# Three rounds of sixteen experts on one core: gate and up weights stored one behind the other, modulation loads spread over twelve experts, tokens' weights computed behind the first expert's rows

## The chip, the cores and the metric

The kernel runs on 1 core of one Trainium2 chip. All data are float32. The metric is the device time of one execution in microseconds (us), lower is better.

## The reference

`x` is 512 tokens of 1024 features. A first block (gated delta rule, spatial gating unit, output projection, layer norm) is followed by a hierarchical mixture of experts; a second model of two layers follows, each with an attention mixer (forgetting attention, then latent attention) and again a mixture of experts. So the mixture of experts runs three times, each time as

```python
def hier_moe(h, w_grp, b_grp, w_rt, b_rt, w_gate, w_up, w_down):
    t = h.reshape(T, D)                                  # 512 x 1024
    g_prob = softmax(t @ w_grp + b_grp)                  # 4 groups, the best is taken
    e_logits = (t @ w_rt + b_rt).reshape(T, 4, 4)        # 4 experts in a group, the two best
    w = softmax(e_top) * g_top                           # two weights per token
    a = einsum('td,edf->tef', t, w_gate)                 # 16 experts, 1024 -> 256
    u = einsum('td,edf->tef', t, w_up)
    hidden = silu(a) * u * combine[..., None]
    return einsum('tef,efd->td', hidden, w_down)         # 256 -> 1024
```

In the second model a layer's six modulation vectors (shift, scale and gate, before and behind the mixer) are `silu(c) @ w_ada + b_ada`, 6 x 1024 values.

## The kernel before, in words

The program is a row of `nc.Block`s. In each of them the five engines (PE for matmuls, DVE, ACT, POOL, and SP, which only issues DMAs) run programs of their own, which wait for one another by semaphores. At the end of a block all five meet: none begins the next block before the last has finished this one, SP included. The trace names such a wait by the line of the block (`PEq L1292` is the one of the mixture of experts).

`moe` (line 1231) is one block with two programs for each engine, one behind the other, with no meeting between them. The first (lines 1293 to 1577) projects the mixer's output, normalises, computes the router's logits and from them, on DVE, which tokens stand in which of 128 slots of each expert: chains of small operations `route`, `pick`, `rows`, and at last `weight` (lines 1524 to 1547), 18 links that wait for one another. `weight` makes each token's two weights `w1`, `w2`, and index lists that are read only behind the experts. It holds two exponentials on ACT (`gexp`, `dif`, lines 1417 to 1420).

The second program goes over the 16 experts, `body(e, par, pair)` for each engine. PE does for expert e: `gate_up` (line 1610, 8 float32 matmuls of 512 columns, gate in columns 0 to 255, up in 256 to 511; the trace counts each float32 matmul twice), then `down` of expert e-1 (line 1619), then `turn_h` (line 1615). The first two experts' rows are turned by PE (`turn_x`, line 1602) and copied from PSUM by ACT and DVE (`keep_x`, line 1626); the others' by DVE (line 1843). POOL fetches an expert's rows in four indirect DMAs of 1 KB pieces (`load_quarters`, line 1875). ACT issues the loads of expert e+2's gate and up weights when `gate_up` of e has ended (`load_gate_up`, line 1788), that of its down weights one step later, and the store of the results of e-1 into `y_rows` (`store_y`, line 1779).

The weights lie in a ring of four slots: `ring[0]` and `ring[1]` take gate and up (4096 floats in each partition), `ring[2]` and `ring[3]` take down. In a partition of `ring[0]` gate and up alternate: for each of 8 values of k, 256 floats of gate and then 256 of up:

```python
act.dma_start(ring[par][:, :].rearrange("p (k g n) -> p k g n", k=KD, g=2)[:, :, i, :],
              w[:, bass.ds(e, 1), :, :].rearrange("p e k n -> p (e k) n"))
```

In DRAM the 8 x 256 floats that a partition takes from one matrix are one run of 8 KB. The load of one matrix therefore writes 8 runs of 1 KB in each partition. The other big loads have runs of 2 KB (`w_in` and the like), 4 KB (down weights) and, for one matrix (`mla_w_ukv`), 8 KB.

SP has little to do during the experts. In the first two of the three rounds it loads what the modulation of the next layer needs (`modulation_loads`, line 1218): small rows, six blocks of 512 KB from `ada_part`, and `ffn_norm`, 512 KB. Each is held back until `gate_up` of one expert has ended: experts 1 to 6 and 7. DVE adds `b_ada` to them at experts 10 to 13 (`BIAS_AT`). Then SP issues the next stage's first two pieces of weights into `ring[0]` and `ring[1]`, behind `gate_up` of experts 14 and 15. The next stage (class `Combine`, line 1911) fetches each token's two results from `y_rows` by indirect DMAs on POOL (line 1971), adds them on DVE (line 2069), sums the modulation on PE (lines 1982 and 1988), normalises, turns the tokens on PE (line 2007) and projects them (line 2363 behind the first round, line 2611 behind the second).

Of the kernel before, what the change touches and what calls it, by code (L numbers as in the profile page):

```python
# [17 lines left out]
ALU = mybir.AluOpType  # L18
# [101 lines left out]
def build(nc, D, OUT, stop=None):  # L120
# [19 lines left out]
    with ctx:  # L140
# [61 lines left out]
        def rows8(w):  # L202
            return w.rearrange("(p k) n -> p k n", p=P)
# [4 lines left out]
        def plan_experts(gate, up, down):  # L208

            for e in range(NE):  # L210
                gu = [(lambda s, i=i: s[:, :].rearrange("p (k g n) -> p k g n", k=KD, g=2)[:, :, i, :], rows8(w[e]))
                      for i, w in enumerate((gate, up))]
                dn = [(lambda s: s[:, 0:KF * DM].rearrange("p (k n) -> p k n", k=KF), rows(down[e]))]
                W.plan(gu, e % 2, by_loop=e >= 2)
                W.plan(dn, 2 + e % 2, by_loop=e >= 2)
# [1015 lines left out]
        def moe(outT, gain, shift, gate_w, up_w, down_w, group_w, group_b, expert_w, expert_b, x_tok, y_in, early, late=None, mod=None):  # L1231
# [47 lines left out]
            dv_n += [("bias", i) for i in range(4)] if mod is not None else []  # L1279
            BIAS_AT = NE - 6  # L1280
            stage([("sum", j) for j in range(6)] + [("turned", 0, 0), ("turned", 0, 1), ("sum", 6), ("turned", 1, 0), ("turned", 1, 1), ("sum", 7)] +
# [10 lines left out]
            with nc.Block() as block:  # L1292
# [89 lines left out]
                def _(act):  # L1382
# [20 lines left out]
                    for t in tiles:  # L1403
# [6 lines left out]
                        if t == 2:  # L1410
# [5 lines left out]
                                                 bcast(ident[:, :].rearrange("p (s n) -> p s n", s=NQ).unsqueeze(2), P, NQ, NQ, P // NQ), ACT.Copy), "spread")  # L1416
                    DV.wait(act, ("weight", 1))
                    AC.done(nc.scalar.activation(gexp, gexp, ACT.Exp), "gexp")
                    DV.wait(act, ("weight", 4))
                    AC.done(nc.scalar.activation(dif, dif, ACT.Exp), "dif")  # L1420

                @block.vector
                def _(dve):
# [99 lines left out]

                    link = chain(DV, dve, "weight")
                    groups = lg3[:, :, 0:NG]
                    gx = gexp.rearrange("p (t n) -> p t n", t=T)
                    link(V.reduce_max(gm, groups, X_AXIS))
                    link(V.tensor_tensor(gx, groups, bcast(gm.unsqueeze(2), P, T, NG), ALU.subtract))
                    link(V.tensor_tensor(four(prod2), four(O12), bcast(lg3[:, :, NG:nrt].unsqueeze(1), P, 2, T, NE), ALU.mult))
                    link(V.reduce_sum(sel, prod2.rearrange("p (a n) -> p a n", n=NE), X_AXIS))  # L1530
                    link(V.tensor_tensor(dif, sel[:, T:2 * T], sel[:, 0:T], ALU.subtract))
                    AC.wait(dve, "gexp")
                    link(V.reduce_sum(gsum, gx, X_AXIS))
                    link(V.reciprocal(gp, gsum))
                    AC.wait(dve, "dif")
                    link(V.tensor_scalar_add(gm, dif, 1.0))
                    link(V.reciprocal(gm, gm))
                    link(V.tensor_tensor(w1, gp, gm, ALU.mult))
                    link(V.tensor_tensor(w2, w1, dif, ALU.mult))
                    c3 = cmpx.rearrange("p (x n) -> p x n", x=N_EXTRA)  # L1540
                    link(V.tensor_tensor(c3, bcast(incl.unsqueeze(1), P, N_EXTRA, NE), bcast(e_idx[:, 0:N_EXTRA].unsqueeze(2), P, N_EXTRA, NE), ALU.is_le))
                    link(V.reduce_sum(eidf[:, 0:N_EXTRA], c3, X_AXIS))
                    link(V.tensor_copy(eidf[:, N_EXTRA:N_EXTRA + 1], incl[:, NE - 1:NE]))
                    link(V.tensor_copy(ctl, eidf))
                    link(V.tensor_scalar(sel, rowsf, float(N_EARLY * P), FAR, ALU.is_lt, ALU.mult))
                    link(V.tensor_tensor(sel, sel, rowsf, ALU.add))
                    link(V.tensor_copy(rows_late, sel))

                @block.gpsimd
# [32 lines left out]
                yg = half(buf[2][:, 0:2048], DM)  # L1582
                w_gu = [ring[i][:, :].rearrange("p (k n) -> p k n", k=KD) for i in range(2)]
                w_dn = [ring[2 + i][:, 0:KF * DM].rearrange("p (k n) -> p k n", k=KF) for i in range(2)]
# [17 lines left out]
                def turn_x(eng, e, par, pair):  # L1602
# [5 lines left out]
                    last.then_inc(M_xT.sem, 1)  # L1608

                def gate_up(e, par):  # L1610
                    for k in range(KD):
                        last = nc.tensor.matmul(bank[2 + par][:, :], xgT[par][:, k, :], w_gu[par][:, k, :], start=(k == 0), stop=(k == KD - 1))  # L1612
                    last.then_inc(M_gu.sem, 1)
# [31 lines left out]
                extra_is = work[:, 3 * 4096 + 2048:3 * 4096 + 2048 + T * P]  # L1645
                extra_gu = halves_of_ring[:, :].rearrange("p (k n) -> p k n", k=KD)
                extra_dn = work[:, 2 * 4096 + 2 * DM:2 * 4096 + 4 * DM].rearrange("p (k n) -> p k n", k=KF)
# [10 lines left out]
                def extra_pe(x):  # L1658
                    nc.tensor.wait_ge(E_is, 2 * T * x + 2 * T)
                    for k in range(KD):  # L1660
                        for t in range(T):
                            last = nc.tensor.matmul(bank[k // 4][:, (k % 4) * P:(k % 4 + 1) * P], eighth(x_tok[:, t, :], k),
                                                    extra_is[:, t * P:(t + 1) * P], start=(t == 0), stop=(t == T - 1))
                    last.then_inc(E_pe, 1)
                    nc.tensor.wait_ge(E_in, 48 * x + 48)
                    nc.tensor.wait_ge(E_act, 3 * x + 1)
                    nc.tensor.wait_ge(E_dve, 4 * x + 1)
                    for k in range(KD):
                        last = nc.tensor.matmul(bank[2][:, :], xgT[0][:, k, :], extra_gu[:, k, :], start=(k == 0), stop=(k == KD - 1))
                    last.then_inc(E_pe, 1)  # L1670
                    nc.tensor.wait_ge(E_dve, 4 * x + 2)
                    for k in range(KF):
                        last = nc.tensor.transpose(bank[4][:, k * P:(k + 1) * P], h_tok[0][:, k * P:(k + 1) * P], ident[:, :])
                    last.then_inc(E_pe, 1)
                    nc.tensor.wait_ge(E_dve, 4 * x + 3)
                    for h in range(2):
                        for k in range(KF):
                            last = nc.tensor.matmul(bank[5 + h][:, :], hT[0][:, k, :], extra_dn[:, k, span(h)], start=(k == 0), stop=(k == KF - 1))
                    last.then_inc(E_pe, 1)

                def extra_act(x):
                    e = nc.scalar.value_load(ctl[0:1, bass.ds(x, 1)], min_val=0, max_val=NE - 1)
                    row = bass.ds(x * P + N_MAIN * P, P)
                    for i, w in enumerate((gr, ur)):
                        nc.scalar.dma_start(halves_of_ring[:, :].rearrange("p (k g n) -> p k g n", k=KD, g=2)[:, :, i, :],
                                            w[:, bass.ds(e, 1), :, :].rearrange("p e k n -> p (e k) n")).then_inc(E_in, 16)
# [71 lines left out]
                @block.sync  # L1758
                def _(sp):
                    W.issue(sp)  # L1760
                    assert W.issued == ids[4]
                    W.issued += 2 * NE - 4
                    if mod is not None:
                        DV.wait(sp, ("weight", N_WEIGHT - 1))
                        modulation_loads(sp, mod, lambda i: sp.wait_ge(M_gu.sem, v(M_gu, i + 1)))
                    W.issue(sp, 2)
                mod_loads = loads[0]

                @block.scalar
                def _(act):  # L1770
# [17 lines left out]
                    def load_gate_up(e, par):  # L1788
                        for i, w in enumerate((gr, ur)):
                            act.dma_start(ring[par][:, :].rearrange("p (k g n) -> p k g n", k=KD, g=2)[:, :, i, :],  # L1790
                                          w[:, bass.ds(e, 1), :, :].rearrange("p e k n -> p (e k) n")).then_inc(W.landed[par], 16)
# [4 lines left out]
                    def body(e, par, pair, first=False, free=False, no_y=False, tail=False, last=False):  # L1796
# [15 lines left out]
                        if not first:  # L1812
                            store_y(e - 1, 1 - par)
                    keep_x_act(0, 0)
                    body(0, 0, 0, first=True, free=True)
                    body(1, 1, 0, free=True, no_y=True)
# [9 lines left out]
                @block.vector  # L1826
                def _(dve):
                    def keep_y_dve(e, par, pair, early=False):
                        dve.wait_ge(M_down.sem, v(M_down, e))
# [16 lines left out]
                    def body(e, par, pair, first=False, early=False, last=False):  # L1846
# [10 lines left out]
                        if mod is not None and BIAS_AT <= e < BIAS_AT + 4:  # L1857
# [3 lines left out]
                            DV.done(nc.vector.tensor_tensor(part, part, b_ada[32 * i:32 * i + 1, :], ALU.add), ("bias", i))  # L1861
                    keep_x_dve(0, 0)
                    body(0, 0, 0, first=True)
                    body(1, 1, 0, early=True)
# [1057 lines left out]
```

## Time and profile before

| | before |
|---|---|
| runs | 2174.18, 2176.12, 2182.51 us; median 2176.12 |
| profiled execution | 2177.57 us, span 2175.8 us |
| mean granted TensorE clock | 0.977 |
| PE busy | 2073.0 us (95%) |
| DVE / ACT / POOL busy | 964.6 / 488.3 / 273.9 us |
| DMA | 363.32 MB in 208486 packets; mean 167 GB/s |

The profile is of the profiled execution. Idle PE time is not the whole loss in this kernel: a matmul at the lower of the clock's two levels counts as busy.

### The profile page before, as it was taken

The numbers are of one execution on the slowest core, as the hardware profiler recorded it, in microseconds if no ns is written. First come the engines' busy times: TensorE is split into PE (matmuls) and PEld (weight loads), VectorE is DVE, ScalarE is ACT, GpSimd is POOL, SyncE is SP. The second block draws the span as 40 slices with busy tenths as digits, with TensorE's granted clock in tenths as the row PEclk, the third lists the DMA queues.
The fourth block names the chain that finished last, engine by engine and source line by source line (L and its number), as shares of the span: only waits on it lengthen the run. The fifth ranks groups of instructions, "written<-read, shape, count | busy, mean of one in ns | idle before, by whom it ended". The sixth has DMA issues, their size and how long they took to land. (4 is left out here: it accounts for less than half of the span.)

```text
span 2175.8 us, 20699 instructions
## 1 busy us (share of the span) xinstructions
PE 2073.0 (95%) x7718; PEld 1159.7 (53%) x7718; DVE 964.6 (44%) x1696; ACT 488.3 (22%) x1086; POOL 273.9 (13%) x348
## 2 busy tenths in 40 slices
PE   8999999999999999999899999989999999999995
PEld 4444445488884445444445468544445568644442
DVE  2445445445553124334454656253353467434333
ACT  1111111043441001101331146220004446420000
POOL 1000000010002000334200000013331000003333
PEclk9999999999999999999998999999999999999998
DMA  5223365410012124799735920148994120045996
GB/s 174 93 94 126 135 245 217 156 41 2 1 53 102 65 92 155 253 376 379 267 121 199 323 111 1 39 144 307 374 379 164 62 98 2 3 153 172 369 374 258
DMA packets 208486, 363.32 MB, mean 167 GB/s; under 512 B 27580, under 2 KB 129240, under 8 KB 208128
## 3 DMA queue, kind: packets, MB, share of 16 engines
q1 hardware_dynamic: 87568, 174.13, 22.9%
q10 hardware_dynamic: 105696, 157.30, 20.5%
q0 software_dynamic: 15120, 30.53, 4.1%
q8 instruction: 64, 1.05, 0.2%
q14 instruction: 38, 0.31, 0.0%
HBM read 335.60 MB, written 43.52 MB: 174 GB/s over the span
## 5 line engine op out<-in xcount | busy, mean ns | idle before, releaser
L1612 PE MATMUL bank<-ring,work 128*128 128x512 f32 x768 | 345.7, 604 | 21.7 <-DVE work L1628 11.6
L1612 PEld LDWEIGHTS bank<-ring,work 128*128 128x128 f32 x768 | 145.0, 194 | 189.8 <-issue 177.1
L1877 POOL DMA_INDIRECT work<-x_rows,small x168 | 172.9, 1029 | 288.9 <-DVE work L1843 212.6
L1623 PE MATMUL bank<-ring_halves,work 128*128 128x512 f32 x384 | 172.9, 593 | 4.0 <-DVE work L1637 4.0
L423 PE MATMUL bank<-featT,ring 128*128 128x512 f32 x384 | 171.3, 600 | 4.3 <-DMA ring<-in_w_in 4.3
L1313 PE MATMUL bank<-ring,work 128*128 128x512 f32 x384 | 171.3, 607 | 2.9 <-PEq L2139 1.9
L2363 PE MATMUL bank<-ring,featT 128*128 128x512 f32 x384 | 169.9, 604 | 1.6 <-DVE small L2452 1.6
L1634 DVE TENSOR_TENSOR work<-work,bank 128x256 f32<-128x256 f32 x48 | 20.2, 421 | 306.0 <-ACT work L1631 306.0
L2363 PEld LDWEIGHTS bank<-ring,featT 128*128 128x128 f32 x384 | 74.1, 195 | 94.3 <-issue 92.5
L1313 PEld LDWEIGHTS bank<-ring,work 128*128 128x128 f32 x384 | 74.1, 195 | 94.0 <-issue 94.0
L1623 PEld LDWEIGHTS bank<-ring_halves,work 128*128 128x128 f32 x384 | 72.9, 190 | 94.9 <-issue 94.9
L423 PEld LDWEIGHTS bank<-featT,ring 128*128 128x128 f32 x384 | 72.3, 193 | 86.6 <-issue 82.3
L1631 ACT ACTIVATE work<-bank 128x256 f32<-128x256 f32 x48 | 18.4, 383 | 429.0 <-PE bank L1612 429.0
L522 PE MATMUL bank<-ring,featT 128*128 128x512 f32 x256 | 110.4, 593 | 0.9 <-PEq L405 0.9
L2197 PEld LDWEIGHTS bank<-work,featT 128*128 128x128 f32 x640 | 88.6, 192 | 24.8 <-issue 14.4
L2189 PE MATMUL bank<-work 65*128 65x128 f32 (+7 forms) x256 | 90.4, 438 | 0.1
L2197 PE MATMUL bank<-work,featT 128*128 128x65 f32 x640 | 86.0, 265 | 0.1
L1843 DVE STREAM_TRANSPOSE work<-work 128x1024 f32<-128x1024 f32 x42 | 85.1, 2025 | 0.0
L1030 PE MATMUL bank<-ring,featT 128*128 128x512 f32 x192 | 83.3, 593 | 1.0 <-PEq L796 1.0
L522 PEld LDWEIGHTS bank<-ring,featT 128*128 128x128 f32 x256 | 48.6, 190 | 61.3 <-issue 61.3
L279 DVE SCALAR_TENSOR_TENSOR ring_halves<-ring_halves,ismall 128x1024 f32<-128x1024 f32 x48 | 61.6, 1282 | 30.2 <-DMA ring_halves<-in_w_ada 26.4
L2215 ACT ACTIVATE featT<-bank,small 128x128 f32<-128x128 f32 (+3 forms) x128 | 73.2, 572 | 5.0 <-DVE small L2252 2.7
(442 smaller groups left out, 2784.8 us busy)
## 6 DMA issues: line engine op xcount, KB each, us to landing
ring<-in_w_in SPq DMA_DIRECT2D x16, 2048.0 KB, 12.6
ring<-in_moe_w_gate ACTq DMA_DIRECT2D x28, 1024.0 KB, 8.6
ring<-in_moe_w_up ACTq DMA_DIRECT2D x28, 1024.0 KB, 11.9
ring_halves<-in_moe_w_down ACTq DMA_DIRECT2D x28, 1024.0 KB, 12.0
ring_halves<-in_w_ada SPq DMA_DIRECT2D x48, 512.0 KB, 6.7
y_rows<-work ACTq DMA_DIRECT2D x48, 512.0 KB, 10.3
ring<-in_expert_w_gate ACTq DMA_DIRECT2D x14, 1024.0 KB, 9.8
ring<-in_expert_w_up ACTq DMA_DIRECT2D x14, 1024.0 KB, 12.8
```

Source lines behind the costliest of these rows:

```text
L423: last = nc.tensor.matmul(bank[b % 4][:, :], w[:, k, (b % 4) * P:(b % 4 + 1) * P], featT[:, k, :], start=(k == 0), stop=(k == KD - 1))
L522: last = nc.tensor.matmul(uv_bank(j)[:, :], featT[:, k, t * P:(t + 1) * P], w[:, k, :], start=(k == 0), stop=(k == KD - 1))
L1030: last = nc.tensor.matmul(zg_bank(j)[:, :], featT[:, k, t * P:(t + 1) * P], w[:, k, :], start=(k == 0), stop=(k == KD - 1))
L1313: last = nc.tensor.matmul(bank[j % 4][:, :], outT[:, k, t * P:(t + 1) * P], w[:, k, :], start=(k == 0), stop=(k == KD - 1))
L1612: last = nc.tensor.matmul(bank[2 + par][:, :], xgT[par][:, k, :], w_gu[par][:, k, :], start=(k == 0), stop=(k == KD - 1))
L1623: last = nc.tensor.matmul(bank[5 + h][:, :], hT[par][:, k, :], w_dn[par][:, k, span(h)], start=(k == 0), stop=(k == KF - 1))
L1843: nc.vector.transpose(xgT[par].rearrange("p k (s b) -> p s k b", s=NQ), xg[par].rearrange("p (s a k) -> p s k a", s=NQ, k=KD)).then_inc(M_ ...
L1877: nc.gpsimd.indirect_dma_start(out=xg[par][:, s * QD:(s + 1) * QD], out_offset=None, in_=x_quarters, in_offset=bass.IndirectOffsetOnAxis(a ...
L2189: PE.done(nc.tensor.matmul(bank[i % N_S][:, 0:(t + 1) * P], qT[:, t * P:(t + 1) * P], kT[:, 0:(t + 1) * P], start=True, stop=True), ("S", i))
L2197: last = nc.tensor.matmul(bank[6 + h % 2][:, t * DVO:(t + 1) * DVO], pT[j % 2][:, s, :], v[:, s, h, :], start=(s == 0), stop=(s == t))
L2215: AC.done(nc.scalar.activation(sx[i % 4][:, 0:n], bank[i % N_S][:, 0:n], ACT.Exp, bias=mx[:, i:i + 1], scale=1.0 if q_root is None else q_ ...
L2363: last = nc.tensor.matmul(f_bank(j)[:, :], featT[:, k, t * P:(t + 1) * P], w[:, k, :], start=(k == 0), stop=(k == KD - 1))
```

## The change

Three things. Gate and up are stored one behind the other in a slot (2048 floats of gate, then 2048 of up), so a matmul's moving operand is two runs of 256 floats that lie 2048 floats apart, and a load writes one run of 8 KB in each partition. The modulation loads are held back to experts 1, 2, 4, 6, 7, 9 and 11 (before: 1 to 7), the additions of `b_ada` to experts 12 to 15, and the second of the next stage's two pieces is issued only when the last result of the odd experts has been stored. The chain `weight` with its two exponentials moves from the first program's end into the second, behind `keep_x` of expert 0.

```diff
@@ plan_experts
-                gu = [(lambda s, i=i: s[:, :].rearrange("p (k g n) -> p k g n", k=KD, g=2)[:, :, i, :], rows8(w[e]))
+                gu = [(lambda s, i=i: s[:, :].rearrange("p (g k n) -> p g k n", g=2, k=KD)[:, i, :, :], rows8(w[e]))
@@ moe
-            BIAS_AT = NE - 6
+            BIAS_AT = NE - 4
@@ moe, first program of ACT
-                    DV.wait(act, ("weight", 1))
-                    AC.done(nc.scalar.activation(gexp, gexp, ACT.Exp), "gexp")
-                    DV.wait(act, ("weight", 4))
-                    AC.done(nc.scalar.activation(dif, dif, ACT.Exp), "dif")
@@ moe, first program of DVE
-                    link = chain(DV, dve, "weight")
-                    groups = lg3[:, :, 0:NG]
...
-                    link(V.tensor_copy(rows_late, sel))
@@ moe, gate_up
-                w_gu = [ring[i][:, :].rearrange("p (k n) -> p k n", k=KD) for i in range(2)]
+                w_gu = [ring[i][:, :].rearrange("p (g k n) -> p k g n", g=2, k=KD) for i in range(2)]
+                gu_sum = [bank[2 + i][:, :].rearrange("p (g n) -> p g n", g=2) for i in range(2)]
-                        last = nc.tensor.matmul(bank[2 + par][:, :], xgT[par][:, k, :], w_gu[par][:, k, :], start=(k == 0), stop=(k == KD - 1))
+                        last = nc.tensor.matmul(gu_sum[par], xgT[par][:, k, :], w_gu[par][:, k, :, :], start=(k == 0), stop=(k == KD - 1))
@@ moe, SP beside the experts
-                        modulation_loads(sp, mod, lambda i: sp.wait_ge(M_gu.sem, v(M_gu, i + 1)))
-                    W.issue(sp, 2)
+                        modulation_loads(sp, mod, lambda i: sp.wait_ge(M_gu.sem, v(M_gu, 1 + 5 * i // 3)))
+                    W.issue(sp, 1)
+                    if W.issued < len(W.chunks):
+                        sp.wait_ge(y_stored[1], all_stored)
+                        W.issue(sp, 1)
@@ moe, load_gate_up
-                            act.dma_start(ring[par][:, :].rearrange("p (k g n) -> p k g n", k=KD, g=2)[:, :, i, :],
+                            act.dma_start(ring[par][:, :].rearrange("p (g k n) -> p g k n", g=2, k=KD)[:, i, :, :],
@@ moe, second program of ACT
                     keep_x_act(0, 0)
+                    DV.wait(act, ("weight", 1))
+                    AC.done(nc.scalar.activation(gexp, gexp, ACT.Exp), "gexp")
+                    DV.wait(act, ("weight", 4))
+                    AC.done(nc.scalar.activation(dif, dif, ACT.Exp), "dif")
                     body(0, 0, 0, first=True, free=True)
@@ moe, second program of DVE
+                    def weights_of_tokens():
...
                     keep_x_dve(0, 0)
+                    weights_of_tokens()
                     body(0, 0, 0, first=True)
```

`weights_of_tokens` holds the 18 links unchanged. The same change of layout is made where a ninth and further blocks of rows of an expert are handled (`extra_pe`, `extra_act`); no such block occurs in the trace.

The instructions of DVE around the start of the experts, first round, before. L1546 and L1547 are the last links of `weight`, L1628 is `keep_x`, L1634 the product with up:

```order
L1545 TENSOR_SCALAR small<-small 128x8 [waits dve_steps]
L1546 TENSOR_TENSOR small<-small 128x8 [waits dve_steps]
L1547 CAST ismall<-small 128x8 [waits dve_steps]
L1826 UNCONDITIONAL_BRANCH [waits dve_steps]
L1628 COPY work<-bank 128x512 [waits moe_x_turned]
L1634 TENSOR_TENSOR work<-work,bank 128x256 [waits moe_silu]
L1628 COPY work<-bank 128x512 [waits moe_x_turned]
```

And DVE at the same place in the changed kernel, where L1518 ends `part_rows`, L1601 is `keep_x`, L1815 to L1835 is `weight` and L1607 the product with up:

```order
L1516 TENSOR_SCALAR work<-bank,small 128x64 [waits pe_steps,dve_steps]
L1518 CAST small<-work 128x64 [waits dve_steps]
L1806 UNCONDITIONAL_BRANCH
L1601 COPY work<-bank 128x512 [waits moe_x_turned]
L1815 TENSOR_REDUCE small<-work 128x4
L1816 TENSOR_TENSOR work<-work,small 128x16 [waits dve_steps]
L1817 TENSOR_TENSOR work<-work 128x128 [waits dve_steps]
L1818 TENSOR_REDUCE small<-work 128x8 [waits dve_steps]
```

All 18 links stand behind the copy that PE waits for; the first product with up stands behind all of them. On ACT the two exponentials likewise stand between L1601 and the load of the table for silu.

The DMAs of SP at the end of the first round, before (the first row is the last of the modulation loads), up to the meeting of the engines:

```order
L185 DMA work<-ada_part 128x1024 [waits moe_gate_up_sum] x5
L185 DMA featT<-in_ffn_norm 128x1024 [waits moe_gate_up_sum]
L116 DMA ring<-in_fox_w_in 128x8x512 [waits moe_gate_up_sum] x2
L2325 UNCONDITIONAL_BRANCH [waits barrier_Pool_Activation_PE_DVE_SP_release]
L185 DMA small<-in_fox_q_norm 64x1
```

And in the changed kernel:

```order
L185 DMA work<-ada_part 128x1024 [waits moe_gate_up_sum] x5
L185 DMA featT<-in_ffn_norm 128x1024 [waits moe_gate_up_sum]
L116 DMA ring<-in_fox_w_in 128x8x512 [waits moe_gate_up_sum]
L116 DMA ring<-in_fox_w_in 128x8x512 [waits moe_gate_up_sum,moe_y_stored1]
L2315 UNCONDITIONAL_BRANCH [waits barrier_Pool_Activation_PE_DVE_SP_release]
```

SP now waits for a store to DRAM ahead of the meeting of all engines, at the end of the first two rounds; the third has no next piece and no such wait.

## Rows read from the trace of the kernel before

**Rows 1.** Waits of line 1612, all three rounds: releaser, us in total, times

```profile
  DMA ring<-in_moe_w_up: 11.4, 11
  DMA ring<-in_expert_w_up: 11.2, 10
```

**Rows 2.** Timeline, start of round one: start, us, engine, line, [idle before <-releaser]

```profile
872.55 0.16 DVE L1527 TENSOR_REDUCE small<-work 128x4 f32<-128x16 f32 x1
873.19 1.16 PE L1607 MATMUL bank<-ident,work 128*128 128x128 f32 x8 [1.18 <-DMA work<-x_rows,ismall]
877.06 0.69 DVE L1628 COPY work<-bank 128x512 f32<-128x512 f32 x1 [0.25 <-DVE ismall L1547]
```

**Rows 3.** PE's timeline: the first gate_up of rounds one, two and three

```profile
877.85 9.35 PE L1612 MATMUL bank<-ring,work 128*128 128x512 f32 x16 [3.50 <-DVE work L1628]
1465.70 8.98 PE L1612 MATMUL bank<-ring,work 128*128 128x512 f32 x16 [3.54 <-DVE work L1628]
1976.51 9.57 PE L1612 MATMUL bank<-ring,work 128*128 128x512 f32 x16 [3.54 <-DVE work L1628]
```

**Rows 4.** Windows: us, busy of five engines, granted clock, DMA share, GB/s

```profile
877.80:888.00 10.20, 10.15 (x24) 4.86 (x24) 0.35 (x1) 0.38 (x1) 1.99 (x2) 0.78 0.09 12
2040.00:2092.00 52.00, 52.00 (x129) 23.39 (x128) 19.51 (x25) 1.92 (x5) 19.95 (x20) 1.00 1.07 373
```

**Rows 5.** PE's timeline: gate_up of experts 4, 10 (round one), 4, 11 (round two)

```profile
920.55 7.03 PE L1612 MATMUL bank<-ring,work 128*128 128x512 f32 x16
990.01 7.03 PE L1612 MATMUL bank<-ring,work 128*128 128x512 f32 x16
1508.02 7.03 PE L1612 MATMUL bank<-ring,work 128*128 128x512 f32 x16
1588.31 7.06 PE L1612 MATMUL bank<-ring,work 128*128 128x512 f32 x16
```

**Rows 6.** Windows of 1 us: gate and up alone (1 KB), mla_w_ukv alone (8 KB)

```profile
824.00:825.00 1.00, 1.00 (x4) 0.49 (x3) 0.00 (x0) 0.00 (x0) 0.00 (x0) 1.00 1.10 354
1702.00:1703.00 1.00, 1.00 (x4) 0.57 (x3) 0.00 (x0) 0.00 (x0) 0.00 (x0) 1.00 0.98 418
```

**Rows 7.** DMA view, last number us to landing: windows 1987:2008, 2092:2113, 921:945

```profile
ring<-in_moe_w_up ACTq DMA_DIRECT2D x3, 1024.0 KB, 9.8
...
ring<-in_moe_w_up ACTq DMA_DIRECT2D x3, 1024.0 KB, 12.5
...
ring<-in_expert_w_up ACTq DMA_DIRECT2D x3, 1024.0 KB, 15.9
```

**Rows 8.** Timeline, experts' rows: turned on DVE, fetched by POOL, and their landing

```profile
1008.35 2.02 DVE L1843 STREAM_TRANSPOSE work<-work 128x1024 f32<-128x1024 f32 x1
1016.32 0.99 POOL L1877 DMA_INDIRECT work<-x_rows,small  x1 [0.31 <-issue]
DMA to landing us min/median/max: 5.7/5.9/9.2
```

**Rows 9.** Timeline: an early meeting, and the ends of rounds one and two

```profile
438.10 0.38 SPq L116 DMA_DIRECT2D ring<-in_w_in  x1
439.12 1.06 PE L811 MATMUL bank<-ident,work 128*128 128x128 f32 x8 [1.05 <-PEq L628]
1058.73 0.34 ACTq L1782 DMA_DIRECT2D y_rows<-work  x1
1060.71 5.39 PE L1982 MATMUL bank<-work,ones 128*128 128x512 f32 x12 [2.79 <-PEq L1292]
1078.45 1.94 PE L2007 MATMUL bank<-ident,work 128*128 128x128 f32 x8 [3.65 <-ACT work L2034]
1649.15 7.09 PE L1982 MATMUL bank<-work,ones 128*128 128x512 f32 x12 [2.84 <-PEq L1292]
1663.13 1.94 PE L2007 MATMUL bank<-ident,work 128*128 128x128 f32 x8 [0.83 <-issue]
```

**Rows 10.** DMA view, 2145:2155, third round's last stores: us to landing

```profile
y_rows<-work ACTq DMA_DIRECT2D x2, 512.0 KB, 3.0
```

More of the change, by code:

```diff
@@ L1522, in _ @@
                     DV.done(V.tensor_copy(part_rows, part_f), "part_rows")
-                    link = chain(DV, dve, "weight")
-                    groups = lg3[:, :, 0:NG]
[L1526 to L1546, printed above, removed]
-                    link(V.tensor_copy(rows_late, sel))
                 @block.gpsimd
@@ L1645, in moe @@
                 extra_is = work[:, 3 * 4096 + 2048:3 * 4096 + 2048 + T * P]
-                extra_gu = halves_of_ring[:, :].rearrange("p (k n) -> p k n", k=KD)
+                extra_gu = halves_of_ring[:, :].rearrange("p (g k n) -> p k g n", g=2, k=KD)
                 extra_dn = work[:, 2 * 4096 + 2 * DM:2 * 4096 + 4 * DM].rearrange("p (k n) -> p k n", k=KF)
@@ L1668, in extra_pe @@
                     for k in range(KD):
-                        last = nc.tensor.matmul(bank[2][:, :], xgT[0][:, k, :], extra_gu[:, k, :], start=(k == 0), stop=(k == KD - 1))
+                        last = nc.tensor.matmul(gu_sum[0], xgT[0][:, k, :], extra_gu[:, k, :, :], start=(k == 0), stop=(k == KD - 1))
                     last.then_inc(E_pe, 1)
@@ L1684, in extra_act @@
                     for i, w in enumerate((gr, ur)):
-                        nc.scalar.dma_start(halves_of_ring[:, :].rearrange("p (k g n) -> p k g n", k=KD, g=2)[:, :, i, :],
+                        nc.scalar.dma_start(halves_of_ring[:, :].rearrange("p (g k n) -> p g k n", g=2, k=KD)[:, i, :, :],
                                             w[:, bass.ds(e, 1), :, :].rearrange("p e k n -> p (e k) n")).then_inc(E_in, 16)
@@ L1827, in _ @@
                 def _(dve):
+                    def weights_of_tokens():
+                        lg3 = lg.rearrange("p (t n) -> p t n", t=T)
+                        four = lambda a: a.rearrange("p (i t n) -> p i t n", i=2, t=T)
+                        V = nc.vector
+                        link = chain(DV, dve, "weight")
+                        groups = lg3[:, :, 0:NG]
+                        gx = gexp.rearrange("p (t n) -> p t n", t=T)
+                        link(V.reduce_max(gm, groups, X_AXIS))
+                        link(V.tensor_tensor(gx, groups, bcast(gm.unsqueeze(2), P, T, NG), ALU.subtract))
+                        link(V.tensor_tensor(four(prod2), four(O12), bcast(lg3[:, :, NG:nrt].unsqueeze(1), P, 2, T, NE), ALU.mult))
+                        link(V.reduce_sum(sel, prod2.rearrange("p (a n) -> p a n", n=NE), X_AXIS))
+                        link(V.tensor_tensor(dif, sel[:, T:2 * T], sel[:, 0:T], ALU.subtract))
+                        AC.wait(dve, "gexp")
+                        link(V.reduce_sum(gsum, gx, X_AXIS))
+                        link(V.reciprocal(gp, gsum))
+                        AC.wait(dve, "dif")
+                        link(V.tensor_scalar_add(gm, dif, 1.0))
+                        link(V.reciprocal(gm, gm))
+                        link(V.tensor_tensor(w1, gp, gm, ALU.mult))
+                        link(V.tensor_tensor(w2, w1, dif, ALU.mult))
+                        c3 = cmpx.rearrange("p (x n) -> p x n", x=N_EXTRA)
+                        link(V.tensor_tensor(c3, bcast(incl.unsqueeze(1), P, N_EXTRA, NE), bcast(e_idx[:, 0:N_EXTRA].unsqueeze(2), P, N_EXTRA, NE), ALU.is_le))
+                        link(V.reduce_sum(eidf[:, 0:N_EXTRA], c3, X_AXIS))
+                        link(V.tensor_copy(eidf[:, N_EXTRA:N_EXTRA + 1], incl[:, NE - 1:NE]))
+                        link(V.tensor_copy(ctl, eidf))
+                        link(V.tensor_scalar(sel, rowsf, float(N_EARLY * P), FAR, ALU.is_lt, ALU.mult))
+                        link(V.tensor_tensor(sel, sel, rowsf, ALU.add))
+                        link(V.tensor_copy(rows_late, sel))
                     def keep_y_dve(e, par, pair, early=False):
```

## The prediction

> **What bounds the kernel now.** I read the page first: PE is busy 95% of the span, so time can only come from PE's few pauses and from stretches in which it runs at the lower level of its clock. The waits of `gate_up` book 22.6 us to the landing of up weights [rows 1]; PE's weight loads are in that sum too, so it counts a stall twice, and the timeline has to tell its true length. The timeline of PE shows a second kind of pause, at each round's start.
>
> **At the start.** PE has turned expert 0's rows at 873.19 + 1.16 = 874.35 [rows 2]. Its `gate_up` needs them copied out of PSUM, and DVE's half of the copy starts at 877.06, because DVE works through the chain `weight` from 872.55 on [rows 2]. PE pauses 3.50 us, and 3.54 in each of the other two rounds [rows 3]. Behind the pause the 16 matmuls take 9.35, 8.98 and 9.57 us [rows 3] where they otherwise take 7.03 [rows 5]; the granted clock of that stretch is 0.78 [rows 4], a mixture of 1.2 and 2.4 GHz. So the pause is paid a second time.
>
> **Late weights** stand in rounds one and two alone. Round three, without modulation loads, runs 52 us without a pause, though its DMA share is 1.07 at 373 GB/s [rows 4]: the queues are never empty, they just keep up. In its steady part one expert takes 10.52 us (PE's own work). In round one the way from expert 4 to expert 10 takes 990.01 - 920.55 = 69.46 us where six experts need 63.12; in round two from 4 to 11 it takes 1588.31 - 1508.02 = 80.29 where seven need 73.64 [rows 5]. That is 6.3 + 6.7 = 13.0 us lost to late weights. The DMA view shows how it builds up: up weights land 9.8 us after issue in a quiet stretch, 15.9 us where the modulation loads run [rows 7].
>
> **The sum, term by term**, against the profiled execution (2177.57 us, 1.45 above the median of the runs).
>
> **1. `weight` behind `keep_x`: -8.1 us.** DVE is free when PE has turned expert 0's rows, so its copy starts 0.04 us behind 874.35, as ACT's does, and lasts 0.69 [rows 2]; with about 0.1 to wake PE, `gate_up` starts at 875.18 instead of 877.85. That is 2.67 us, and 3.54 - 0.83 = 2.71 in the other rounds. The chain takes 877.06 - 0.25 - 872.55 = 4.26 us [rows 2], and now runs from 875.1 to 879.4. What hides it is `gate_up` of expert 0, to 875.18 + 7.03 = 882.2; DVE next waits for silu behind that. If the cover were gone it would cost 4.26 each time; its slack is 2.8. ACT's two exponentials fall into the same cover. Who else waits for `weight`: SP's small modulation loads (its queue has nothing else then) and POOL's early gathers, at expert 12. Nothing is lost there. `part_rows`, for which POOL waits, stays ahead.
>
> **2. The clock across that start: -5.8 us.** At 7.03 us each the three first `gate_up` would give back 2.32 + 1.95 + 2.54 = 6.8 us [rows 3, 5]. What is left before them are pauses of 1.18 us [rows 2] and 0.83 us with turns between. The nearest row is at a stage's end: after 2.79 us of pause the 12 matmuls of line 1982 still take 5.39, at the upper level, while after 2.84 in round two they take 7.09 [rows 9]. So pauses of nearly 3 us cost something in one of two cases; the two short ones should cost less. I take 85% of 6.8. The ends are 0 and 6.8.
>
> **3. Runs of 8 KB, and spread modulation loads: -12.0 us.** Alone in the queues, gate and up in runs of 1 KB move at 354 GB/s in the window shown; the one matrix with 8 KB runs moves at 418 [rows 6]. By this ratio the 2.1 MB of an expert's gate and up take 5.9 us before and 5.0 now, 0.9 less of DMA time in each expert's 10.52. What a round lacks today is the 6.5 us of stalls and the 15.9 - 9.8 = 6.1 us by which the landing slips before PE stalls at all [rows 7], 12.6 together. Two parts make it up: seven modulation blocks of 0.52 MB at 373 GB/s, 1.4 us each, 9.8 in all, and the small lack that round three shows too, where the landing goes from 9.8 to 12.5 over some twelve experts [rows 7], 0.2 each. The new runs give back 0.9 for each expert, so over the twelve experts between first and last block 9.8 + 12 x 0.2 - 12 x 0.9 = 1.4 us are lacking, which the 6.1 of slip take up. The stalls go; I leave 1.0 us of 13.0 for fetches and stores that fall together. Spreading alone would change little: with the old runs the same 12 us are lacking in the end. If the rate did not rise at all, this term is 0; nothing gives more than 13.0.
>
> The Trainium skill (DMA: Bandwidth & Descriptors, section "Where 436 GB/s comes from") speaks against this term: for transfers from DRAM it gives a limit per core of about 358 GB/s on the DRAM side, whatever the run length. The trace disagrees, with 373 over 52 us [rows 4] and 418 [rows 6]. By that rule alone the term would be 0 and the sum 12 us higher.
>
> **4. Split moving operand: 0.** No matmul of the trace reads two runs of 256. The nearest is line 1607, whose operand is read with a stride of 8 floats: 8 turns in 1.16 us, of which about 0.1 is start-up. It bounds the price from above at some hundredths for each expert. From below nothing: the operand's length is the same.
>
> **5. SP's wait for the last store: +3.5 us.** All engines meet behind the experts, and SP now comes last. An uncontended store lands 3.0 us after issue [rows 10]. From SP's issue of a load to PE's first matmul behind a meeting it is 439.12 - 438.10 = 1.02 us [rows 9]. Round one: store issued at 1058.73, so PE starts at 1058.73 + 3.0 + 1.0 = 1062.8 instead of 1060.71, 2.1 late. PE had 3.65 us of slack there, waiting for ACT [rows 9], and ACT's path begins with the gathers, which need that same store and so are not later (they may be earlier, since the 2 MB piece no longer competes with the store): +0.5. Round two: there PE does not wait at line 2007 (0.83, issue alone) [rows 9]; its sums are the path. It starts some 2.7 later, and a longer pause may cost clock: +3.0. The ends are -1 (earlier gathers) and +9 (both rounds in full with 2.4 us of lower clock each). The late pieces are needed behind the turns at 1078.45 and 1663.13 [rows 9], 17 and 11 us after their issue, and 2 MB at 373 GB/s take 5.6: nothing waits for them.
>
> **6. `b_ada` at experts 12 to 15: 0.** One operation of DVE each, in the time in which DVE waits for silu.
>
> Sum: -8.1 - 5.8 - 12.0 + 3.5 = -22.4, so 2155.2 for a run like the profiled one and 2153.7 against the median; I say 2154.
>
> **Rivals.**
> *Large runs starve the rows.* POOL's fetches of an expert's rows are of 1 KB pieces, 8 to a DMA engine for each fetch, and would now wait behind 8 KB instead of 1 KB of weights. The last fetch is issued at 1016.32 and lands 5.9 later, at 1022.2; DVE turns the rows two experts behind 1008.35, at 1029.4 [rows 8]. So the mechanism decides from a landing of 13.1 us on. With one 8 KB run ahead of each piece, 8 x 9 KB at 418/16 GB/s is 2.8 us instead of 0.7, so 8 us to land: hidden. If a whole engine's share of a load (64 KB, 2.5 us) passed between two pieces, a fetch would take some 20 us, 7 too many over two experts, 3.5 us in each of some 40 experts. Then it is slower; at 16 us (1.45 for each of 42 experts, +61) the time would be 2215, and the gain is used up at 14.2 us. The Trainium skill (same page, "Queues, rings and completion order") says that each DMA engine goes round its queues packet by packet, a packet being some 9 to 17 descriptors; that is nearer the bad case. Against it: today's fetches land in 5.9 us beside saturated queues [rows 8]. Chance 0.05.
> *The rate does not rise* (the 8 KB row is of a load that ran alone, the experts' queues are shared by stores and 4 KB runs). Then -8.1 - 5.8 + 3.5 = -10.4, or 2165.7. Chance 0.09.
> *The end costs in full, and the clock is not regained*: -8.1 - 0 - 12 + 9 = -11, 2165. Chance 0.07.
> My forecast with its neighbours, 2147 to 2163: 0.79.
>
> **How the numbers follow.** A measurement of this kernel can tell about 0.5% (10.9 us, 2165.2) from no change. The two middle rivals lie on that line; half of their 0.16 goes to "same", and a little more of the forecast's tail: faster 0.85, same 0.10, slower 0.05. The range goes from 2147 (all stalls and all clock gained, the end free: -8.1 - 6.8 - 13 - 1 = -29) to 2166, which takes in both middle rivals.
>
> **What would show it.** In the changed profile: the pauses before the first `gate_up` 0.8 us, and these at 7.0 to 7.6 us; packets down by some 80,000; DMA share with 390 GB/s or more in the loaded part; no start later than 10.6 us behind the last; up weights landing in under 11 us; PE's pause at both meetings near 5 us. It would be wrong if experts 5 to 10 still waited for up weights, if DVE waited for rows at the turning, or if the meetings cost more than 5 us each.

## The result, and the profile after

The changed kernel takes 2153.39 us (median of 5 runs, 2150.46 to 2159.08) against 2176.12 (5 runs, 2174.18 to 2182.51): a ratio of 0.990, interval 0.9876 to 0.9924. The forecast was 2154. Measured again beside four other kernels it took 2154.68 (6 runs) against 2172.09 (11 runs), ratio 0.9913 (0.990 to 0.9927). So the gain is about 20 us.

The page of the changed kernel, lines from several of its parts:

```profile
PEclk9999999999999999999999999999999999999998
DMA  5223365510003224699636830048993120035996
DMA packets 122470, 363.32 MB, mean 169 GB/s; under 512 B 27580, under 2 KB 30936, under 8 KB 109824
L1585 PE MATMUL bank<-ring,work 128*128 128x512 f32 x768 | 343.8, 601 | 3.3 <-DVE work L1601 3.3
L1852 DVE STREAM_TRANSPOSE work<-work 128x1024 f32<-128x1024 f32 x42 | 85.1, 2026 | 0.0
```

The same bytes go in 122470 packets instead of 208486. `gate_up` (now line 1585) waits for nothing but `keep_x`; the landing of up weights, which stood in its waits before [rows 1], is gone. DVE's turns of the experts' rows (line 1852) never waited for a row.

PE's timeline at the starts of the three rounds (start, us, line, idle before):

```profile
872.01 1.16 PE L1578 MATMUL bank<-ident,work 128*128 128x128 f32 x8 [1.30 <-DMA work<-x_rows,ismall]
874.00 8.60 PE L1585 MATMUL bank<-ring,work 128*128 128x512 f32 x16 [0.83 <-DVE work L1601]
1451.06 8.50 PE L1585 MATMUL bank<-ring,work 128*128 128x512 f32 x16 [0.83 <-DVE work L1601]
1953.09 10.06 PE L1585 MATMUL bank<-ring,work 128*128 128x512 f32 x16 [0.83 <-DVE work L1601]
```

The pause is 0.83 instead of 3.5 us in each round [rows 3], as worked out. But the first `gate_up` still takes 8.5 to 10.1 us. Windows of 1 us of the changed kernel there (us; busy time of PE, of its weight loads, of DVE, ACT and POOL; granted clock, DMA share, GB/s):

```profile
872.00:873.00 1.00, 0.98 (x8) 0.97 (x8) 0.00 (x0) 0.00 (x0) 0.00 (x0) 1.00 0.79 303
873.00:874.00 1.00, 0.17 (x2) 0.03 (x1) 0.77 (x2) 0.60 (x1) 0.00 (x0) 0.80 0.18 74
874.00:875.00 1.00, 1.00 (x2) 0.48 (x3) 0.89 (x4) 0.21 (x1) 0.98 (x1) 0.50 0.01 4
...
877.00:878.00 1.00, 1.00 (x3) 0.41 (x3) 0.86 (x5) 0.00 (x0) 0.69 (x2) 0.99 0.32 94
```

The clock still falls to its lower level (0.50, 1.2 GHz), now in the second half of the shorter pause, and comes back at 877. Summed over the rounds, the three `gate_up` take 27.16 us where they took 27.90 [rows 3]: 0.7 us came back, and the forecast had 5.8.

Windows: first the kernel before, from the start of expert 4 to that of expert 10 in round one; then the changed kernel over the same six experts, from there to the last `down`, and across the meeting to the second projection behind it (line 2373):

```profile
920.55:990.01 69.46, 64.45 (x158) 28.59 (x157) 20.31 (x25) 5.88 (x12) 23.93 (x24) 1.00 1.07 378
...
915.95:979.07 63.12, 63.12 (x158) 28.39 (x157) 20.33 (x25) 5.88 (x13) 23.93 (x24) 1.00 1.02 407
979.07:1043.30 64.23, 63.29 (x158) 28.35 (x157) 24.61 (x29) 6.46 (x13) 20.40 (x18) 1.00 0.97 381
1043.30:1080.46 37.16, 30.80 (x94) 15.79 (x95) 22.08 (x29) 17.75 (x32) 9.08 (x8) 0.86 0.50 179
```

Six experts take 63.12 us, six times 10.52, where they took 69.46 [rows 5]; PE is busy all of it and the DMA engines move 407 GB/s instead of 378. Round two takes 73.65 for seven experts instead of 80.29. The two rounds' stalls of 13.0 us are gone to the last. The higher rate shows where gate and up move alone too, ahead of round one, in the window of [rows 6] (354 GB/s there):

```profile
824.00:825.00 1.00, 1.00 (x4) 0.49 (x3) 0.00 (x0) 0.00 (x0) 0.00 (x0) 1.00 0.97 406
```

Around the meeting behind round one, and PE's first work behind the two meetings:

```profile
1047.79 0.34 ACTq L1758 DMA_DIRECT2D y_rows<-work  x1
1050.86 0.38 SPq L116 DMA_DIRECT2D ring<-in_fox_w_in  x1
1051.68 6.79 PE L1992 MATMUL bank<-work,ones 128*128 128x512 f32 x12 [4.71 <-PEq L1292]
...
1630.36 7.58 PE L1992 MATMUL bank<-work,ones 128*128 128x512 f32 x12 [5.83 <-PEq L1292]
```

The store is issued at 1047.79, SP issues its piece 3.07 us later, and PE goes on 0.82 behind that: a pause of 4.71 instead of 2.79, and 5.83 instead of 2.84 in round two. The 12 matmuls behind it take 6.79 us instead of 5.39, and 7.58 instead of 7.09 [rows 9].

### The profile page after: what moved, and what is told of

The parts are those of the page before. It is cut to its first block and busy times, and to the rows that moved or that the text cites. A ratio compares the mean times of both kernels' runs of the same rounds, so it can differ in the third digit from the quotient of the medians.

```text
span 2151.7 us, 20701 instructions
## 1 busy us (share of the span) xinstructions
PE 2066.1 (96%) x7718; PEld 1154.6 (54%) x7718; DVE 964.7 (45%) x1696; ACT 488.4 (23%) x1086; POOL 271.0 (13%) x348
## 2 busy tenths in 40 slices
DMA packets 122470, 363.32 MB, mean 169 GB/s; under 512 B 27580, under 2 KB 30936, under 8 KB 109824
## 5 line engine op out<-in xcount | busy, mean ns | idle before, releaser
L1607 DVE TENSOR_TENSOR work<-work,bank 128x256 f32<-128x256 f32 x48 | 20.2, 421 | 283.6 <-ACT work L1604 283.6
L522 PEld LDWEIGHTS bank<-ring,featT 128*128 128x128 f32 x256 | 48.5, 190 | 61.5 <-issue 61.4
```

The source lines that it names most:

```text
L522: last = nc.tensor.matmul(uv_bank(j)[:, :], featT[:, k, t * P:(t + 1) * P], w[:, k, :], start=(k == 0), stop=(k == KD - 1))
```

## The experiments

Each was timed in five rounds beside the kernel before on the same chip. A ratio is to that; a difference in us behind it is worked out from the ratio and the time of before, and lies within about 2 us of the difference of the two medians.

**One part of the change at a time.** `layout_alone` is the kernel before with only the layout:

```diff
-  rearrange("p (k g n) -> p k g n", k=KD, g=2)[:, :, i, :]        # both loads of a slot
+  rearrange("p (g k n) -> p g k n", g=2, k=KD)[:, i, :, :]
-  nc.tensor.matmul(bank[2 + par][:, :], xgT[par][:, k, :], w_gu[par][:, k, :], ...)
+  nc.tensor.matmul(gu_sum[par], xgT[par][:, k, :], w_gu[par][:, k, :, :], ...)
```

> The kernel before with the new layout of gate and up alone; modulation loads, weight chain and the next stage's pieces as before. Theory (longer runs end the stalls by themselves): no gate_up of rounds one and two starts later than about 10.6 us behind the last, and the time falls by 12 to 14 us, to about 2163. Rival (the stalls went because the modulation loads were spread): most of the 13.0 us of late weights stay, up weights still land some 15 us after issue in the loaded part, and the time falls by at most 4 us.

Measured: 2159.32 (6 runs) against 2174.37 (29 runs), ratio 0.994 (0.992 to 0.996), 13.0 us faster. The window of its trace from expert 4 to expert 13 of round one:

```profile
917.98:1012.83 94.85, 94.85 (x236) 42.63 (x235) 33.88 (x39) 8.83 (x19) 38.30 (x36) 1.00 1.02 404
```

Nine experts in 94.85 us where PE's own work is 94.68, so 0.2 us of stalls are left, though the modulation loads stand at experts 1 to 7. The queues move 404 GB/s. The longer runs are enough by themselves.

`spread_alone`:

```diff
-  lambda i: sp.wait_ge(M_gu.sem, v(M_gu, i + 1))
+  lambda i: sp.wait_ge(M_gu.sem, v(M_gu, 1 + 5 * i // 3))
-  BIAS_AT = NE - 6
+  BIAS_AT = NE - 4
```

> The kernel before with the modulation loads held back to experts 1, 2, 4, 6, 7, 9, 11 and the additions of b_ada at experts 12 to 15, nothing else. Theory: the same bytes at the same rate lack as much in the end; the stalls move to later experts and sum to 10 to 13 us as before, the time is within 3 us of the kernel before. Rival: the stalls shrink to under 3 us and the time falls by 10 or more.

Measured: 2173.03 (12 runs) against 2174.37, ratio 0.9999 (0.9985 to 1.0013): nothing. The waits of `gate_up` over all rounds, and the first and last of the five long stalls of round one:

```profile
  DMA ring<-in_expert_w_up: 10.6, 10
  DMA ring<-in_moe_w_up: 10.5, 10
```

```profile
941.04 7.13 PE L1612 MATMUL bank<-ring,work 128*128 128x512 f32 x16 [0.99 <-DMA ring<-in_expert_w_up]
1019.71 7.13 PE L1612 MATMUL bank<-ring,work 128*128 128x512 f32 x16 [0.89 <-DMA ring<-in_expert_w_up]
```

21.1 us in that view instead of 22.6 [rows 1]; by the timeline, eleven experts take 122.02 and 122.07 us in the two rounds where 115.7 is PE's own, 12.6 us lost instead of 13.0. Each stall is now beside a later load. Holding loads back moves a lack of transfer time, it does not remove it.

`weight_alone` moves the chain `weight` and its exponentials as the change does, and nothing else.

> The kernel before with the chain weight and its two exponentials moved behind keep_x of expert 0, nothing else. By the term of the sum: three pauses of 0.83 us instead of 3.5, 8.1 us. What the trace of the changed kernel adds: the clock still falls there, so the whole gain is 8 to 9 us (2167 to 2168); by the prediction's term for the clock it would be 14 (2162).

Measured: 2164.92 (12 runs), ratio 0.9959 (0.9947 to 0.9971), 8.9 us faster. The pauses are 0.83 us, the three first `gate_up` 8.77, 8.74 and 10.11. It is the pauses' 8.1 us and nothing of the clock.

`late_piece_alone`:

```diff
-  W.issue(sp, 2)
+  W.issue(sp, 1)
+  if W.issued < len(W.chunks):
+      sp.wait_ge(y_stored[1], all_stored)
+      W.issue(sp, 1)
```

> The kernel before with only the second piece of the next stage's weights issued behind the last store of the odd experts. By the sum's term: slower by 3.5 us (bounds -1 and +9), PE's pause at the meetings of rounds one and two about 5 us instead of 2.8. Rival (the store and the gathers, freed of the 2 MB piece, give back what the meeting loses): no difference, and the first projection behind each meeting starts as early behind the last down as before.

Measured: 2175.47 (12 runs), ratio 1.0013 (1.0000 to 1.0025), 2.8 us slower (1.1 by the medians), with 0 at the interval's edge. SP, PE and POOL behind round one, and PE behind round two:

```profile
1061.68 0.38 SPq L116 DMA_DIRECT2D ring<-in_fox_w_in  x1
1062.51 7.53 PE L1985 MATMUL bank<-work,ones 128*128 128x512 f32 x12 [4.71 <-PEq L1292]
1063.28 0.98 POOL L1974 DMA_INDIRECT work<-y_rows,ismall  x1 [25.18 <-POOLq L1292]
...
1649.40 7.63 PE L1985 MATMUL bank<-work,ones 128*128 128x512 f32 x12 [6.22 <-PEq L1292]
```

The pauses are 4.71 and 6.22, and behind both the 12 matmuls take 7.5 us, part of them at the lower clock. POOL now waits for the meeting (`POOLq L1292`) and no longer for the store. The four parts add up to -13.0 - 0.2 - 8.9 + 2.8 = -19.3 us, and the whole was measured at -22 and -19.

**What the wait for the store costs in the changed kernel.** `changed_again` is the changed kernel; `no_late_piece` has `W.issue(sp, 2)` again; `second_piece_next_block` leaves the second piece to the next block's SP, whose first line issues it.

> The changed kernel as it is, on the chip of the next three, to compare them with it. About 2153.

> The changed kernel with the next stage's second piece issued behind gate_up of expert 15, as before the change. By late_piece_alone (a meeting 1.9 and 3.4 us later, the first projection behind it about 1 and 2 us later): 3 us faster than the changed kernel, bounds 0 and 5. Rival (with long runs in the queues the 2 MB piece holds up the last down weights and the store more than the wait costs): as fast or slower than the changed kernel.

> The changed kernel with the second piece issued as SP's first act behind the meeting, with no wait ahead of it. PE's pause at both meetings is 2.8 us again, and the store has the queues to itself. If the meeting is what costs: 3 us faster than the changed kernel, like no_late_piece; if the piece beside the gathers costs too, less than that.

Measured, all against 2172.09: 2154.68 (0.9913), 2150.02 (0.990, 0.9885 to 0.9914) and 2152.36 (0.9897, 0.9881 to 0.9913). The medians put both variants 2 to 5 us ahead of the changed kernel, but the intervals overlap, so the times alone don't settle it. The traces say more: from the start of the last `down` of round one to that of the second projection behind the meeting it is 37.2, 37.2 and 37.0 us in the three kernels that wait (`late_piece_alone`, the changed kernel twice) and 36.4, 36.1, 34.2, 37.2, 34.1 and 34.5 in six that don't. (These six are the kernel before, `spread_alone`, `layout_alone`, `weight_alone`, `no_late_piece` and `clock_filled`.) Behind round two, to the fifth projection, it is 48.5, 48.1 and 50.1 against 45.8, 45.8, 48.3, 48.7, 43.5 and 47.5. That is 1.7 and 2.3 us in the mean, 4.0 in all, with a scatter of the same size; with the four traces of the kernels below, which don't wait either (33.2 to 36.5 and 47.4 to 48.8), it is 2.0 and 1.8. In `second_piece_next_block` the pauses are 2.77 and 2.82 us again, but the second projection stands 37.3 behind the last `down`: there the piece costs beside the gathers what the meeting saves. Behind round two its fifth projection stands at 45.9, as early as in kernels that don't wait, so one trace doesn't settle it.

**The clock.** `clock_filled` is `no_late_piece` with two dummy matmuls more in each round. A dummy matmul writes a bank of PSUM that nobody reads. The kernel before has such matmuls already, in waits earlier in the stage (line 1345).

```diff
                     PE.done(last, "parts")
+                    nc.tensor.matmul(bank[5][:, :], ident[:, :], x_tok[:, 0, 0:BANK], start=True, stop=True)
@@ second program of PE
                     turn_x(pe, 0, 0, 0)
+                    nc.tensor.matmul(bank[5][:, :], ident[:, :], x_tok[:, 0, 0:BANK], start=True, stop=True)
                     body(0, 0, 0, first=True)
```

> no_late_piece with two dummy matmuls of 512 columns more on PE in each round: one while PE waits for expert 0's rows (1.3 us), one while it waits for keep_x (0.83 us). If the clock falls there because of these two pauses, the first gate_up takes 7.1 us instead of 8.5 to 10.1 in all three rounds, and the kernel is 4 to 6 us faster than no_late_piece. If the pauses earlier in the stage (0.3 us each, and the short matmuls of 16 to 80 columns) are what lowers it, the first gate_up still takes 8.5 or more and the time is the same or 0.3 us longer.

Measured: 2140.97 (2139.71 to 2147.85), ratio 0.9866 (0.9849 to 0.9883); 9.0 us faster than `no_late_piece` by the medians, 7.4 by the ratios. PE's timeline at the start of its round one:

```profile
870.74 1.10 PE L1381 MATMUL bank<-resid,ident 128*128 128x512 f32 x2
872.27 1.16 PE L1580 MATMUL bank<-ident,work 128*128 128x128 f32 x8 [0.43 <-DMA work<-x_rows,ismall]
873.27 1.02 PE L1719 MATMUL bank<-resid,ident 128*128 128x512 f32 x2
874.27 7.11 PE L1587 MATMUL bank<-ring,work 128*128 128x512 f32 x16
```

The dummy matmuls (L1381 and L1719) fill the pauses, and `gate_up` takes 7.11 us; 7.10 and 7.11 in the other rounds. In `no_late_piece` it was 8.78, 10.12 and 8.80. That is 6.4 us of the gain, which is larger than the 4 to 6 expected. The two profiled executions differ by 9.5 us, and the other 3.1 lie where the two kernels are the same.

Which of the two pauses matters? One dummy matmul at a time:

> no_late_piece with one dummy matmul of 512 columns, between the turns of expert 0's rows and its gate_up (the 0.83 us pause); the wait for the rows stays unfilled. If this pause decides, the first gate_up takes 7.1 us in all rounds and the time is that of clock_filled, 2141; if both pauses count together, some of the three still take 8.5 or more, and the time lies between 2141 and 2150.

> no_late_piece with one dummy matmul of 512 columns while PE waits for expert 0's rows (1.3 us, 0.4 left); the 0.83 us pause stays. If the longer pause decides, as clock_filled; if the 0.83 us pause decides, the first gate_up still takes 8.5 to 10.1 and the time is that of no_late_piece, 2150.

Measured against 2173.15: 2144.61, ratio 0.9865 (0.9846 to 0.9883), and 2142.37, ratio 0.9862 (0.9845 to 0.988). Both are like `clock_filled`; since filling either pause is enough for that time, neither of the two readings that blamed a single pause holds. With the 0.83 us pause left, all three first `gate_up` take 7.1 us (rounds one and three):

```profile
872.92 1.16 PE L1580 MATMUL bank<-ident,work 128*128 128x128 f32 x8 [0.21 <-DMA work<-x_rows,ismall]
874.91 7.11 PE L1587 MATMUL bank<-ring,work 128*128 128x512 f32 x16 [0.83 <-DVE work L1603]
...
1939.42 1.10 PE L1381 MATMUL bank<-work,ident 128*128 128x512 f32 x2
1941.89 1.16 PE L1580 MATMUL bank<-ident,work 128*128 128x128 f32 x8 [1.36 <-DMA work<-x_rows,ismall]
1943.88 7.10 PE L1587 MATMUL bank<-ring,work 128*128 128x512 f32 x16 [0.83 <-DVE work L1603]
```

With the wait for the rows left, two take 7.11 and the third 7.78, behind a wait of 1.52 us:

```profile
1946.51 1.29 PE L1578 MATMUL bank<-ident,work 128*128 128x128 f32 x8 [1.52 <-DMA work<-x_rows,ismall]
1947.60 1.91 PE L1717 MATMUL bank<-work,ident 128*128 128x512 f32 x2
1949.31 7.78 PE L1585 MATMUL bank<-ring,work 128*128 128x512 f32 x16
```

There the clock was at its lower level under the dummy matmul (1.91 us instead of 1.02) and came back at 1950.7, 1.4 us into `gate_up`. So one dummy matmul in either pause gives back all or most of the clock's cost, and one ahead of the turns is enough in all three rounds. The lengths of the pauses that are left don't explain it alone: in round three with the dummy matmul ahead of the turns (above, last three rows) a wait of 1.36 us remains behind the dummy matmul and 0.83 behind the turns, as long as in the changed kernel (1.31 and 0.83 in round three, 10.06 us), and the clock holds. What decides stays open.

> The kernel before with its pauses at each round's start filled: one dummy matmul while PE waits for expert 0's rows, four behind the turns, where it waits 3.5 us for the chain weight. Nothing else. The first gate_up takes 7.1 us instead of 9.0 to 9.6: 6 to 7 us in all. If that is the clock's whole share, about 6 us faster than the kernel before (2166 to 2168); clock_filled was 9 us faster than no_late_piece, so if the missing 3 us come from the filling too, it is 9.

`before_filled` (one dummy matmul before the turns, four behind them, where the kernel before waits for `weight`) took 2169.51 (12 runs), ratio 0.9979 (0.9966 to 0.9992), 4.6 us faster, interval 1.7 to 7.4. Its first `gate_up` take 7.11, 7.11 and 7.03, 6.6 us less than before [rows 3]. The time fell by 2 us less than that; the 9 us that were the other expectation lie outside the interval. So 6.8 us was the right size for what the clock costs at the rounds' starts, and it could be had without the change.

> clock_filled with the modulation loads at experts 1 to 7 again. Theory (long runs suffice, the spread does nothing): same time as clock_filled, 2141 within 3 us, and no gate_up of rounds one and two more than 10.7 us behind the last. Rival (with the start 4 us earlier the slack is gone and the stalls return): 3 us slower or more.

Measured: 2149.35 (2144.68 to 2150.42), ratio 0.9884 (0.9865 to 0.9903). By the medians that is 8 us behind `clock_filled`, by the ratios 4; both are outside the 3 us expected. Its trace shows far less in the rounds: three `gate_up` come 10.70 to 10.88 us behind the last and two 10.62 and 10.63, where the steady step is 10.52: 1.0 us lost in both rounds together. Two of them are later than the 10.7 expected. Its profiled execution is 10.8 us longer; nearly all the rest lies ahead of round one (876.2 us to the first turn, against 872.3) and between the rounds, where the two kernels are the same. The intervals of the two ratios overlap. So the spread is worth about 1 us here; whether it is more stays open.

## Why the prediction was right, and where not

The time (2154 for 2153.4) came out closer than its terms. One by one:

1. *`weight` behind `keep_x`, -8.1.* Right: three pauses of 0.83 us, and -8.9 (6.3 to 11.5) for `weight_alone`. DVE's chain and ACT's exponentials stayed under the first `gate_up`.
2. *The clock across the start, -5.8.* Wrong. In the changed kernel's trace the three `gate_up` give back 0.7 us. Over the fifteen of the five kernels with 0.83 us of pause and no filling they take 9.12 us in the mean; over the twelve of the four with about 3.5 us (in two cases 3.28 and 2.29) it is 9.03: nothing regained. The step that failed was to read two short pauses as cheaper than one of 2.8 us (row 1060.71 of [rows 9]). In these fifteen cases 1.0 to 1.8 and 0.83 us were left ahead of `gate_up`, with only eight turns between, and thirteen of them lost the clock; two kept it (7.11 us). Why those two did stays open. The term's upper end, nothing, was close to the value.
3. *Runs of 8 KB, -12.0.* Right in size and in mechanism: all 13.0 us of stalls went, `layout_alone` gave 13.0 (8.7 to 17.4) and `spread_alone` 0.2, as "spreading alone would change little" said. The rate of the loaded stretch went from 378 to 407 GB/s, and down weights, whose landing the profile still gives, landed 10.7 us after issue between 921 and 945 instead of 14.5. The first and the last modulation block stand ten experts apart, not twelve; with ten the sum of the term lacks 9.8 + 2.0 - 9.0 = 2.8 us instead of 1.4, still less than the 6.1 of slip. With the blocks at experts 1 to 7, six apart, it lacks 9.8 + 1.2 - 5.4 = 5.6 us (an estimate by the same prices), just under 6.1, and there 0.2 us (`layout_alone`) and 1.0 us (`filled_not_spread`) of stalls were left. The figure of the Trainium skill that was weighed there (DMA: Bandwidth & Descriptors, "Where 436 GB/s comes from", about 358 GB/s for a core's transfers from DRAM) is worked out there as half of a stack's rate, for two cores. This kernel runs on one core, and the limit did not bind: the measured 407 GB/s decide.
4. *Split moving operand, 0.* Right: 16 matmuls in 7.03 us before and after.
5. *The wait for the last store, +3.5.* About right in size, and shown only weakly: +2.8 (0 to 5.4) alone, 3.8 to 4.0 by the mean stretches behind the meetings, 0.7 + 2.3 = 3.0 in the profiled executions of before and after.
6. *Starved fetches* did not come: DVE's turns waited for no row. The landing times of weights and rows are not given by the profile for the 8 KB loads, so whether up weights landed in under 11 us was not seen.

The corrected terms make -8.1 - 0.7 - 13.0 + 3.0 = -18.8 us. The profiled executions differ by 24.1 (2175.8 - 2151.7). The other 5.3 us lie where nothing was changed: 1.2 ahead of round one, 1.7 and 1.2 between the rounds, 1.2 at the end. The second measurement of the changed kernel, 17.4 by the medians and 18.9 by the ratio, agrees with the corrected sum. So the forecast's -22.4 was 3.6 us too much: 5.1 too much for the clock, less 1.0 too little for the stalls and 0.5 too much cost at the meetings. The scatter of the first measurement, of which those 5.3 us are a part, covered it: that 2154 came so close to 2153.4 is luck.

## What to carry to other kernels

Where DMA queues are never empty, count the transfer time that a stretch lacks and look at the length of the runs first: storing two matrices one behind the other instead of interleaved ended nearly all stalls by itself, while moving other loads to later steps ended none. A wait for a DMA in a program that must meet the others holds up all of them (PE's pause went from 2.79 to 4.71 us), even on an engine that is otherwise idle. When a pause ahead of a long run of matmuls is shortened, look whether the clock holds; if not, try one dummy matmul in the remaining pause: here it gave back 6.4 us in three rounds, beside the 8.1 of the shorter pauses. `clock_filled`, 2140.97 us, has the lowest median of the kernels here, 31 us below the kernel before by the medians and 29 by the ratio; the two kernels with one of its dummy matmuls are level with it.

## What was not expected of the hardware

One dummy matmul (shown as x2 in the rows) of 1.10 us in a pause of 1.3 us held TensorE at 2.4 GHz through a following pause of 0.83 us, and with its like in the other rounds saved 6.4 us. Without it the clock was at 0.50 for 3.3 to 6.7 us (873.6 to 877 in round one; 1952.4 to 1959.1 in round three of the changed kernel) though each of PE's pauses was shorter than the one of 2.79 us behind which the kernel before ran at full speed. DMA engines at a share of 1.07 with gate and up in 1 KB runs had 8% more to give with 8 KB runs: 378 to 407 GB/s in mixed traffic.
